# Expert gathers of four picks of 32 tokens in place of two picks of 64 (or one of 128), on one Trainium2 core

## The reference

```python
q = (xb @ wq).reshape(blk, PEER_HEADS, 2, PEER_DK_HALF)
s = jnp.einsum('thpc,hpnc->thpn', q, subkeys).astype(jnp.float32)
sv, si = lax.top_k(s, PEER_TOPK)
...
fv, fi = lax.top_k(cand, PEER_TOPK)
eidx = jnp.take_along_axis(cidx, fi, axis=-1)
gate = jax.nn.softmax(fv, axis=-1)
act = jax.nn.gelu(jnp.einsum('thkd,td->thk', pu[eidx], xb).astype(jnp.float32), approximate=False) * gate
return jnp.einsum('thk,thkd->td', act.astype(xb.dtype), pv[eidx])
```

## Time and profile before

| | us |
|---|---|
| median of 3 runs | 2017.08 (2016.5 to 2019.6) |
| the profiled execution | 2018.31 |
| its span, first to last instruction | 2016.5 |
| PE busy | 1641.0 (81%) |
| DVE busy | 1344.2 (67%) |
| ACT busy | 674.8 (33%) |
| POOL busy | 785.7 (39%) |
| moved by DMA | 723.5 MB, of which the gathers' queue 545.82 MB |

### The profile page before, as it was taken

The page is one execution under the profiler, slowest core; times in us unless marked ns, Lnnn a source line. Parts: engine busy times, 40 slices in busy tenths (PEclk is TensorE's granted clock), DMA queues, the critical chain, the costliest instruction groups (busy, mean ns, idle before and its releaser), DMA issues.

```text
span 2016.5 us, 26382 instructions
## 1 busy us (share of the span) xinstructions
PE 1641.0 (81%) x8436; PEld 890.8 (44%) x8436; DVE 1344.2 (67%) x3101; ACT 674.8 (33%) x1964; POOL 785.7 (39%) x581
## 2 busy tenths in 40 slices
PE   6999997887968897776699777679978788887776
PEld 4445455564755452443355234335533443332223
DVE  4256666644468876766887666688768668776754
ACT  2201232131134452333445333344533333442332
POOL 0087560403014443443444333444434345444441
PEclk9998998988989997888899789979988999999999
DMA  7377757965679999999999999999999999999996
GB/s 309 130 251 261 240 171 253 336 244 178 204 319 416 420 415 423 421 422 420 412 380 400 423 415 422 421 409 399 395 413 420 421 421 419 412 416 421 416 407 275
DMA packets 130469, 723.50 MB, mean 359 GB/s; under 512 B 17072, under 2 KB 18993, under 8 KB 58389
## 3 DMA queue, kind: packets, MB, share of 16 engines
q0 software_dynamic: 75024, 545.82, 65.8%
q1 hardware_dynamic: 55309, 176.00, 24.2%
HBM read 712.77 MB, written 9.09 MB: 358 GB/s over the span
## 4 chain that ended last, share of the span: by engine, by line
PE 38%; DMA 32%; DVE 15%; issue 6%; SPq 4%; ACT 3%; POOL 2%; DVEq 0%; POOLq 0%; ACTq 0%
PE bank L503 37%; DMA R<-in_peer_uv,R 16%; DMA RING<-in_peer_uv,R 13%; DVE RING L2370 4%; SPq L2628 2%; DVE R L2370 2%; SPq L2684 2%; ACT R L1441 1%; DMA R<-in_x_prompt 1%; PE bank L510 1%; POOL R L2557 1%; DMA RING<-out_v_sample 1%; DVE R L2097 1%; ACT R L1451 1%; POOL MV L2557 1%
## 5 line engine op out<-in xcount | busy, mean ns | idle before, releaser
L2614 POOL DMA_INDIRECT RING<-in_peer_uv,R x390 | 442.8, 1135 | 668.4 <-PE bank L503 546.8
L503 PE MATMUL bank<-RING,R 128*64 128x512 f32 (+2 forms) x1560 | 511.0, 661 | 191.3 <-ACT R L1441 187.4
L2370 DVE SCALAR_TENSOR_TENSOR RING<-RING,MV 128x1024 f32<-128x1024 f32 x288 | 351.6, 1223 | 183.3 <-DMA RING<-in_peer_uv,R 172.3
L503 PE MATMUL bank<-R 128*128 128x128 f32 (+6 forms) x2184 | 406.2, 386 | 79.0 <-ACT R L1441 74.3
L503 PEld LDWEIGHTS bank<-R 128*128 128x128 f32 (+3 forms) x2184 | 262.7, 188 | 244.4 <-issue 235.6
L503 PEld LDWEIGHTS bank<-RING,R 128*64 128x64 f32 (+2 forms) x1560 | 157.0, 159 | 445.8 <-issue 433.5
L1451 ACT ACTIVATE R<-R 128x2 f32<-128x2 f32 x256 | 51.9, 203 | 701.1 <-DVE RING L2370 585.7
L2614 POOL DMA_INDIRECT R<-in_peer_uv,R x130 | 150.9, 1161 | 214.8 <-PE bank L503 196.4
L2370 DVE SCALAR_TENSOR_TENSOR RING<-RING,R 128x1024 f32<-128x1024 f32 x96 | 117.3, 1222 | 59.6 <-DMA RING<-in_peer_uv,R 55.0
L2370 DVE SCALAR_TENSOR_TENSOR R<-R,MV 128x1024 f32<-128x1024 f32 x96 | 117.4, 1223 | 54.4 <-DMA R<-in_peer_uv,R 52.8
L503 PE MATMUL bank<-HT,RING 128*128 128x512 f32 x320 | 141.9, 601 | 0.0
(11 more groups left out here) (347 smaller groups left out, 1858.5 us busy)
## 6 DMA issues: line engine op xcount, KB each, us to landing
R<-in_peer_wq SPq DMA_DIRECT2D x12, 2048.0 KB, 11.5
RING<-in_w_mod SPq DMA_DIRECT2D x11, 2048.0 KB, 9.1
R<-in_cache_v SPq DMA_DIRECT2D x84, 256.0 KB, 3.6
MV<-in_cache_k SPq DMA_DIRECT2D x64, 256.0 KB, 4.0
R<-in_cache_k SPq DMA_DIRECT2D x64, 256.0 KB, 3.6
R<-in_w_out SPq DMA_DIRECT2D x6, 2048.0 KB, 15.2
MV<-in_cache_v SPq DMA_DIRECT2D x44, 256.0 KB, 3.9
RING<-in_peer_uv,R POOLq DMA_INDIRECT x390, 12.6
```

The source lines that it names most:

```text
L503: i = nc.tensor.matmul(out, lhsT, rhs, start=start, stop=stop, **k)
L2370: V.scalar_tensor_tensor(u, u, 1.0, H2HIGH if s_ % 2 and n < PAIRED * PH else H2[n // PH % 2], ALU.mult, ALU.mult, accum_out=DOT[:, n % 4, ...
L2614: nc.gpsimd.indirect_dma_start(UV[g % UN], None, a["peer_uv"][0], bass.IndirectOffsetOnAxis(ap=idx, axis=0)).then_inc(S(f"uv_in{g % UN}"), 16)
```

## The change

Every gather of all four tiles brings four picks of 32 tokens: partitions 32a to 32a+31 hold pick a of token block b = step mod 4. The diagonal `DG` is 128 by 32. A pair of steps still makes four products; each now fills one group of 32 columns: in bank `lo` the rows of its own block, in bank `hi` the rows turned by 64, so that the four lie in four different column groups. `value_step` is gone. What reads the sums (`sums_copied`, `sums_out`) turns the upper half back, with three operations in place of two.

The index and gate moves become 16 operations of 32 partitions each, in every unit, in place of 4 (tiles 0 to 2) or 1 (tile 3).

The tokens' rows lie four times, block b repeated in `QUARTER[b]`. They are made per tile by PE (`quarters`: 32 products of 32 columns and 512 elements) and copied by ACT (`quarter`: 8 copies of 128x512), from `HN`, which takes the place of the two `H2` buffers. For tile 0 this stands behind the scores of unit 1 and ahead of the second query piece; for the others it is spread over the last three events of the tile before and the first of the tile. `halves` is gone.

`QUARTER` takes the space of the second half of the first query piece, which is therefore loaded again (1 MB) for tiles 1, 2 and 3, as a new piece in `w_parts`.

On SP, the first five groups of key pages were all issued ahead of the store and the broadcast load of the sample queries; now two are, and the other three follow behind these.

```diff
-PAIRED = 3
...
-        H2 = [part(R2, 10240, 1024), MV[:, 3, :]]
+        HN = part(R2, 10240, 1024)
+        QUARTER = [MV[:, b, :] for b in range(4)]
-        H2HIGH = MV[:, 2, :]
-        FOLD = hide_q[:, 0:64]
+        FOLD = hide_q[:, 0:32]
-        DG = part(R2, 11628, 512, n=4, c=P)
-        DGH = part(R1, 11960, 256, n=4, c=64)
+        DG = part(R1, 11960, 128, n=4, c=32)
-            return H2[t % 2] if t < TILES else HS2[0:NB, :]
+            return HN if t < TILES else HS2[0:NB, :]
...
-            w_parts += [(tile, "wo", c) for c in range(2)] + [(tile, "wq", c) for c in range(1, 4)]
+            w_parts += [(tile, "wo", c) for c in range(2)] + [(tile, "wq", c) for c in range(4)]
...
+        def quarters_at(e):
+
+            n, s_ = step_at(e)
+            if n is None or n >= SAMPLES:
+                return []
+            t, at = divmod(n * STEPS + s_ + 3, PH * STEPS)
+            return [(t, at)] if at < 4 and 0 < t < TILES else []
...
-                    wk = w[:, k, :] if c else WR[k // 4][:, k % 4, :]
+                    wk = w[:, k, :] if c else WR[0][:, k, :] if k < 4 else (w if i else WR[1])[:, k - 4, :]
...
+            def quarters(t, b):
+
+                if t:
+                    pe.wait_ge(S("h_ready"), nth_h2(t) + 1)
+                for half in range(2):
+                    k = take_bank(("quarter", t, b, half), "D")
+                    for to in range(0, P, 32):
+                        mm(k[to:to + 32, :], ident[:, 32 * b:32 * b + 32], HN[:, half * 512:half * 512 + 512],
+                           sem=full(("quarter", t, b, half)) if to == 96 else None)
...
             head_scores(1)
+            pe.wait_ge(S("h_ready"), nth_h2(0) + 1)
+            for b in range(4):
+                quarters(0, b)
...
-                    w = None if c == 0 else w_slot(pe, i, "wq", c) if j == q == 0 else W[w_parts.index((i, "wq", c)) % 2]
+                    w = w_slot(pe, i, "wq", c) if j == q == 0 else W[w_parts.index((i, "wq", c)) % 2]
...
-            def value_step(g, n, s_):
...
-                first, last = h == 0 and s_ == 0, h == PH - 1 and s_ == STEPS - 2
-                if first and t >= 2:
-                    pe.wait_ge(S("sums_taken"), 2 * (t - 1))
+                first, last = h == 0 and s_ < 4, h == PH - 1 and s_ >= STEPS - 4
+                if h == s_ == 0 and t >= 2:
+                    pe.wait_ge(S("sums_taken"), 3 * (t - 1))
                 for b in range(2):
                     pe.wait_ge(S(f"uv_in{(g + b) % UN}"), 16 * ((g + b) // UN + 1))
                 pe.wait_ge(S("diagonal"), k + 2)
-                for bank, at in ((lo, 1024), (hi, 1536)):
+                for bank, at, turn in ((lo, 1024, 0), (hi, 1536, 2)):
                     for b in range(2):
-                        mm(bank[64 * b:64 * b + 64, :], DGH[:, (k + b) % 4, :], UV[(g + b) % UN][:, at:at + 512], first, last,
+                        to = 32 * ((s_ + b + turn) % 4)
+                        mm(bank[to:to + 32, :], DG[:, (k + b) % 4, :], UV[(g + b) % UN][:, at:at + 512], first, last,
                            S("v_used") if bank is hi else None)
...
-            def halves(t):
...
+            def quarter(t, b):
+
                 if t:
-                    act.wait_ge(S("dots"), at_step[t * PH - 1, STEPS - 1] + 1)
-                A(H2HIGH[64:P], high, ACT.Copy).then_inc(S("half_rows"), 1)
-                A(H2HIGH[0:64], high, ACT.Copy).then_inc(S("half_rows"), 1)
-                act.wait_ge(S("half_rows"), 3 * t + 2)
-                A(high, low, ACT.Copy).then_inc(S("half_rows"), 1)
+                    act.wait_ge(S("dots"), at_step[t * PH - 1, STEPS - 4 + b] + 1)
...
-                dst, ones_ = (DGH, FOLD) if n < PAIRED * PH else (DG, ident[:, :])
-                A(dst[:, k % 4, :], ones_, ACT.Copy, scale=AG[:, n % 4, s_:s_ + 1]).then_inc(S("diagonal"), 1)
+                A(DG[:, k % 4, :], FOLD, ACT.Copy, scale=AG[:, n % 4, s_:s_ + 1]).then_inc(S("diagonal"), 1)
...
-                for half in range(2):
-                    A(H2[t % 2][:, half * 512:(half + 1) * 512], banks[(t % 2) * 2 + half][:, :], ACT.Copy).then_inc(S("sums_taken"), 1)
+                lo, hi = banks[(t % 2) * 2], banks[(t % 2) * 2 + 1]
+                A(HN[:, 0:512], lo[:, :], ACT.Copy).then_inc(S("sums_taken"), 1)
+                A(HN[0:64, 512:1024], hi[64:P, :], ACT.Copy).then_inc(S("sums_taken"), 1)
+                A(HN[64:P, 512:1024], hi[0:64, :], ACT.Copy).then_inc(S("sums_taken"), 1)
...
-            step(V.tensor_tensor(FOLD, ident[:, 0:64], ident[:, 64:P], ALU.add))
+            step(V.tensor_reduce(FOLD, ident[:, :].rearrange("p (a c) -> p c a", a=4), AXX, ALU.add))
...
-            blocks = [(a_, b) for a_ in range(2) for b in range(2)]
+            blocks = [(a_, b, slice(32 * a_, 32 * a_ + 32), slice(32 * b, 32 * b + 32)) for a_ in range(4) for b in range(4)]
...
-                for a_, b in blocks:
-                    dst, src_ = slice(64 * a_, 64 * a_ + 64), slice(64 * b, 64 * b + 64)
-                    step(V.scalar_tensor_tensor(eix[dst, lo + b:hi:2], R01[src_, 0, lo + a_:hi:2], float(NKEY), R01[src_, 1, lo + a_:hi:2], ALU.mult, ALU.add))
+                for a_, b, dst, src_ in blocks:
+                    step(V.scalar_tensor_tensor(eix[dst, lo + b:hi:4], R01[src_, 0, lo + a_:hi:4], float(NKEY), R01[src_, 1, lo + a_:hi:4], ALU.mult, ALU.add))
...
-                if n % PH == s_ == 0 and n < UNITS:
-                    if n < PAIRED * PH:
-                        dve.wait_ge(S("half_rows"), 3 * (n // PH) + 3)
-                    else:
-                        dve.wait_ge(S("h_ready"), nth_h2(n // PH) + 1)
+                if n < UNITS and n % PH == 0 and s_ < 4:
+                    dve.wait_ge(S("quarters"), 8 * (n // PH) + 2 * s_ + 2)
...
-                    V.scalar_tensor_tensor(u, u, 1.0, H2HIGH if s_ % 2 and n < PAIRED * PH else H2[n // PH % 2], ALU.mult, ALU.mult, accum_out=DOT[:, n % 4, s_:s_ + 1]).then_inc(S("dots"), 1)
+                    V.scalar_tensor_tensor(u, u, 1.0, QUARTER[s_ % 4], ALU.mult, ALU.mult, accum_out=DOT[:, n % 4, s_:s_ + 1]).then_inc(S("dots"), 1)
...
-                if n >= PAIRED * PH:
-                    step(V.tensor_scalar(GAT[:, x, :], GAT[:, x, :], SUMG[:, x:x + 1], None, ALU.mult))
-                else:
-                    for a_, b in blocks:
-                        dst, src_ = slice(64 * a_, 64 * a_ + 64), slice(64 * b, 64 * b + 64)
-                        step(V.tensor_scalar(GATS[dst, x, b:16:2], GAT[src_, x, a_:16:2], SUMG[src_, x:x + 1], None, ALU.mult))
+                for a_, b, dst, src_ in blocks:
+                    step(V.tensor_scalar(GATS[dst, x, b:16:4], GAT[src_, x, a_:16:4], SUMG[src_, x:x + 1], None, ALU.mult))
...
+                step(V.tensor_tensor(QUARTER[0][:, 0:512], lo[:, :], HN[:, 0:512], ALU.mult))
+                step(V.tensor_tensor(QUARTER[0][0:64, 512:1024], hi[64:P, :], HN[64:P, 512:1024], ALU.mult))
+                step(V.tensor_tensor(QUARTER[0][64:P, 512:1024], hi[0:64, :], HN[0:64, 512:1024], ALU.mult))
...
-            for n in range(3):
-                cache_group("cache_k", n, page_numbers(n))
-            job_done(sp, last_job[3])
-            for n in range(3, 5):
+            for n in range(2):
                 cache_group("cache_k", n, page_numbers(n))
             job_read(sp, ("fq", 4))
             store(samp_d[:, 4, :], PS[0:NB, COL_FQ:COL_FQ + 512], "samp_out")
@@ -2710,6 +2710,9 @@
             job_done(sp, last_job[2])
             for b in range(2):
                 load(QB[:, b, :], samp_d[b:b + 1, 4, :].to_broadcast([P, 512]), f"qb_in{b}")
+            job_done(sp, last_job[3])
+            for n in range(2, 5):
+                cache_group("cache_k", n, page_numbers(n))
             chunk(6)
             for t in range(TILES):
...
-                load(W_ROWS[m % 2], {"wo": w_out, "wq": wq}[name][c], f"w{m % 2}_loaded")
+                if name == "wq" and c == 0:
+                    load(W_ROWS[m % 2][:, 0:2048], wq[0, :, 2048:4096], f"w{m % 2}_loaded")
+                else:
+                    load(W_ROWS[m % 2], {"wo": w_out, "wq": wq}[name][c], f"w{m % 2}_loaded")
...
-                elif kind == "wq" and c and j == 3 and q == 1:
+                elif kind == "wq" and j == 3 and q == 1:
...
```

More of the change, by code:

```diff
@@ L1470, in _ @@
             head_scores_out(1)
-            halves(0)
+            job_done(act, ("qT", 0, 0, 3))
+            job_done(act, ("oT", 4, 0))
+            for b in range(4):
+                quarter(0, b)
             for j in range(4):
@@ L1552, in _ @@
                     post_slot(*slot_)
+                for t, b in quarters_at(e):
+                    quarter(t, b)
                 for t, half in rows_at(e):
```

44 lines of the change are left out of this document (16 added, 28 removed).

## The result

The changed kernel takes 2062.24 us (four runs, 2056.84 to 2069.93); the kernel before took 2016.79 us beside it. The ratio is 1.0226, with a 95% interval of 1.0191 to 1.0260. I had forecast 2024.5 us, and my range ended at 2043. The sign was right. The size was not, and no rival named it either: the worst one stood at 2046.5. The changed kernel's profile is of its fastest execution, 5.4 us under the median, so the traces account for 38.5 of some 45 us.

A forecast was written before the change was run, and what follows sets the result against it. Transfers at about 422 GB/s were taken as the bound. Key pages -4, start +7, reload +7.5, turns 0, delta stretches -1, end -2 gave +7.5 us on 2018.3, less 1.2 to the median: 2024.5 us, range 2006 to 2043.

The forecast's parts named there:

- What bounds the kernel: From 600 us on, transfers at about 422 GB/s; faster engines can return at most 26 us, 16 where the delta rule runs.
- Prices of the parts: Value pairs on PE fall to 1.10 us; small DVE operations cost 0.185 us (index) and 0.25 us (gates) each.
- the reload: Half a query piece loaded again for tiles 1 to 3, 3 x 1.05 MB where DMA is the limit: +7.5 us.
- the turns: At the changes of tile, PE products and ACT copies replace DVE's halves: net 0, bounds -2 and +6 us.
- The end: After the last value pair, a shorter pair against three operations in place of two: -2 us.
- The start of the gathers: First gather 2.2 us later, first dot 9.6, ninth gather 7.9; DMA stands about 5 us: +7 us, bounds +2 and +9.
- Key pages: Before the first gather, an earlier sample-query store removes PE's 4.04 us stall: -4 us, bounds -4 and 0.
- Delta stretches: Three 140 us stretches with the delta rule: DVE's added 18 us and PE's relief nearly cancel, -1 us, bounds -16 and +13.
- My own sign of being wrong: The prediction is wrong if DVE's waits for PE stay at 10 us in each 140 us stretch with the delta rule.
- Rival (b): DVE becomes the bound where the delta rule runs, its waits for PE staying: +23.5 us, 2040.5 us; chance 0.25.
- (a): PE was the true bound and DVE has room, so delta-rule stretches run at full rate: -9.5 us, 2007.5 us; chance 0.23.
- (c): PE gets no relief, as its products don't overlap or its clock falls: +29.5 us, 2046.5 us; chance 0.07.

The follow-up runs named there:

- pages_only: The kernel before with only the key pages reordered, two groups ahead of the sample-query store and three behind the broadcasts: 2005.78 us, ratio 0.9966.
- wide_products: The changed kernel with value products 64 columns wide in two column groups, as before, sums mixing rows: 2098.92 us, ratio 1.0416.
- spread: The changed kernel with its sixteen gate operations four a step over steps 8 to 11 and its sixteen index operations in three parts: 2041.29 us, ratio 1.0145.
- four_blocks: The changed kernel with four operations on 64-row blocks for indices and for gates in place of sixteen each, landing in wrong rows: 2009.54 us, ratio 0.9973.

## Why the prediction failed, step by step

**What bounds the kernel: right.** The transfers do, in quiet stretches, and what a faster engine can give back is only what the delta stretches lose. With four operations and narrow products the first three units of tiles 0 to 2 took 3.6, 2.5 and 1.3 us less than before.

**Prices of the parts: right.** The small operations were 0.160 and 0.244 us (forecast 0.185 and 0.25), a run of sixteen 3.00 and 4.05 us at the start (forecast near 3.0 and 4.0). The Trainium skill's figure in VectorE: DVE Perf Modes, TRN2 errata section, which gave 65 ns as an estimate, is off by two and a half to nearly four times, as the rows of before had said. The pair took 1.07 us at the high clock (forecast 1.10), the reload 8.9 us by the runs (forecast 7.5), the turns 0 (forecast 0). The end gave 1.2 us (forecast 2).

**The start of the gathers: right.** Timeline rows of after, to be laid beside the earlier trace rows:

```profile
573.50 0.99 POOL L2617 DMA_INDIRECT RING<-in_peer_uv,R  x1 [69.88 <-DVEq L2306]
...
591.83 4.05 DVE L2384 TENSOR_SCALAR R<-R 32x4 f32<-32x4 f32 x16
596.10 1.23 DVE L2375 SCALAR_TENSOR_TENSOR RING<-RING,MV 128x1024 f32<-128x1024 f32 x1 [0.22 <-DVE R L2384]
...
599.80 1.93 PE L509 MATMUL bank<-RING,R 128*32 128x512 f32 x8 [14.65 <-ACT R L1446]
...
602.51 1.74 POOL L2617 DMA_INDIRECT RING<-in_peer_uv,R  x1 [19.34 <-PE bank L509]
```

From the first gather to the first dot product 22.6 us in place of 15.1 (+7.5, forecast 7.4), to the ninth gather 29.0 in place of 23.2 (+5.8, forecast 5.7). The rate from 600 to 620 us fell to 291 GB/s, the gap that was forecast.

**Key pages: mechanism right, size off.** Forecast -4, measured -7. The term left out the slow products behind the stall (2.5 us), though the interval of the measurement, 3.6 to 10 us, doesn't exclude 4. I had forecast the first gather at 581.5; it came at 573.5. In pages_only the products behind the stall end 7.4 us earlier (115.07 against 122.48), which explains 3.4 of the 8 us between. The rest I can't explain: under the same order that time lay anywhere from 570.4 to 582.0.

**Delta stretches: the step that failed.** It said that DVE's added 18 us a stretch would go into its waits for gathers and a smaller wait for PE, for -1 us in all. The trace has some 29 us there, the 36.9 of tiles 0 to 2 less 7.5 for the reload. My own sign of being wrong, DVE's waits for PE staying at 10 us a stretch, came true (12.6 in units 8 to 11), and DVE was not at 130 of 140 us but at 84%, since the stretch grew with the work. Three errors lie in it. First, a wait inside a stretch isn't room: waits stand where the order puts them, and the added work stood at steps 8 and in the picks. In units 8 to 11 DVE's idle time didn't shrink from 19.7 us, it grew to 23.0. Second, I let PE's relief of 24 us a stretch cancel DVE's 18. PE's busy time in the three stretches fell by 11.3, 1.0 and 8.7 us only, at a clock of 0.83, 0.75 and 0.77 in place of 0.93, 0.89 and 0.86. What the relief was worth with a loaded DVE, 38 us over the whole kernel, went into a smaller loss: wide_products shows what the change would have cost without it. Third, a run of 4.2 us between the two dot products of a pair goes through ACT, PE and POOL to the gathers one after another, and there is no slack for it: I had written myself that these stretches "cannot be late at all".

**Rival (b)** had the mechanism, DVE as the bound, and its price was too low, 12 us for three stretches. It added DVE's work to waits for PE of 10 us, and dropped everything else. In spread, where its picture holds best, units 8 to 11 take 135.8 us: 9.1 more than before and 11.6 more than with four operations, where it had reckoned 4 for a whole stretch. The right comparison is the time that the same units take with PE relieved and DVE not loaded, since the change gives the one and takes the other.

**Tile 3, unit 24: overlooked.** I gave tile 3 no loss, since the delta rule isn't there. But in unit 24 two parts of the picks are done at each step, and it follows the turn from tile 2. That unit before:

```profile
1658.60:1699.40 40.80, 34.43 (x80) 12.96 (x79) 34.38 (x101) 16.13 (x50) 21.39 (x18) 0.96 1.01 418
```

and after:

```profile
1693.20:1743.20 50.00, 26.38 (x132) 6.43 (x135) 42.78 (x147) 19.28 (x61) 21.34 (x18) 0.67 0.95 379
```

DVE was at 34.4 of 40.8 us already, and got 8.4 more: +9.2 us. With four operations (four_blocks) the unit took 43.3 us. The next unit gave 4.4 us back, and tile 3 as a whole lost 5.1.

**Where the sum agreed by luck.** Without the delta stretches the forecast came to +8.5 us and the two profiles come to about +9, but in that 9 stand 5.1 us of tile 3 that I hadn't forecast and a first gather 8 us earlier than forecast. The sign would have been right by these terms; nearly all of the size is in the term that I had put at -1.

**Rivals (a) and (c).** (a), room on DVE, is refuted. (c) asked for no relief on PE. The clock did fall, to 0.75 in units 8 to 11, further than the 0.90 that I had read from a quiet stretch, and PE's busy time there hardly shrank, from 103.0 to 102.1 us. So its condition came about in this stretch. But four_blocks has nearly the same clock (0.79) at 411 GB/s, so a clock as low as that did not cost the time. What the Trainium skill says in TensorE: Matmul & The Clock Gate, Part 1, that the clock is released by activity, agrees with these rows; no run shows that the loss came from it. Whether the low clock adds something of its own once DVE is late, I can't tell apart: no run kept the clock up with PE's work unchanged.

## What to carry to other kernels

Before adding small operations to an engine, set its work in the fullest stretch against the time that stretch would take with every other bound lifted, and don't count its idle time as a reserve: here DVE was busy 107 of 124 us, and of 15.7 us more work 11.6 were paid even in the better order. Operations that are cheap by their elements cost by their number (sixteen on 32 rows took four times as long as four on 64 rows), and where they stand between two links of a chain they are paid on every engine of it, so put them in small parts or on an engine that has room. When a change bundles an independent improvement, time it alone: here it was the only part worth keeping.

## What the runs showed of the hardware

- A low granted clock on PE went with nearly the full transfer rate where PE had slack: in four_blocks 0.79 in units 8 to 11 at 411 GB/s, and 0.56 from 1700 to 1840 us at 420 GB/s.
- A stall of PE cost more than its length: after 4.04 us of standing, products that take 3.7 us at a granted clock of 1.00 took 6.2 at 0.60.
- The same small operation (32x4, scaled by a value per row) took 0.244 us on DVE and 0.299 us on ACT.
